# Fifth and sixth expert's weights loaded in pieces, three of six ahead of the last normalised rows

## The reference, cut to what matters

```python
h = rms_norm(x) * (1 + scale1) + shift1
q, k, v, gu, gv = split(h @ w_in)
mix = concat(attention(q, k, v), gelu(gu) * spatial(norm(gelu(gv)))) @ w_out
x = x + gate1 * rms_norm(mix)
h2 = rms_norm(x) * (1 + scale2) + shift2
# router: the best of 4 groups, then the best 2 of its 8 experts
gates = top2_weights(h2 @ router_group, h2 @ router_expert)
hid = silu(h2 @ w_gate[e]) * (h2 @ w_up[e])          # e = 0..31, 1024 -> 256
f = sum_e gates[:, e] * (hid @ w_down[e])            # 256 -> 1024
y = x + gate2 * rms_norm(f)
```

## The kernel before, in words

| place | bytes of which | over what it lies |
|---|---|---|
| w_5 gate | b0 .. b0+8 KB | `h2`, the rows being written to DRAM |
| w_5 up | b0+8 .. +16 KB | `pick_c`, `shift_r`, `shift_b`, `res_t`, most of `w_rs` |
| w_5 down | b0+16 .. +24 KB | rest of `w_rs`, `junk_2`, `mix_g` |
| w_6 gate, up | b0+24 .. +40 KB | `st_bc`, `sel_slot`, `code_oh`, `one_hot` and others of the router |
| w_6d | first 8 KB of the gates' region | `gate_bc[:, 0]`, read until the last tile's `mix_g` |

## Time and profile before

### The profile page before, as it was taken

The page is one execution under the profiler, slowest core; times in us unless marked ns, Lnnn a source line. Parts: engine busy times, 40 slices in busy tenths (PEclk is TensorE's granted clock), DMA queues, the critical chain, the costliest instruction groups (busy, mean ns, idle before and its releaser), DMA issues.

```text
span 671.0 us, 9726 instructions
## 1 busy us (share of the span) xinstructions
PE 548.3 (82%) x3055; PEld 301.5 (45%) x3056; DVE 192.8 (29%) x575; ACT 151.3 (23%) x375; POOL 173.5 (26%) x240
## 2 busy tenths in 40 slices
PE   0479999999987789999997789899998878788700
PEld 0235654444354455455554445455554444444300
DVE  1150312001367763244467102011111111111037
ACT  2630102002126663232221011111111111111142
POOL 1000000002513332143335423334332222221212
PEclk9999999999998999999998899999998898899955
DMA  8999108054199300620044959999999999999183
GB/s 254 401 404 397 65 1 312 1 193 183 37 312 409 124 2 1 219 95 31 33 166 143 409 220 407 395 392 408 405 395 401 402 404 393 406 403 395 47 327 157
DMA packets 53192, 170.23 MB, mean 254 GB/s; under 512 B 7660, under 2 KB 8340, under 8 KB 52256
## 3 DMA queue, kind: packets, MB, share of 16 engines
q1 hardware_dynamic: 46112, 155.45, 60.1%
q0 software_dynamic: 6752, 14.13, 5.9%
q10 hardware_dynamic: 288, 0.13, 0.1%
HBM read 163.23 MB, written 14.58 MB: 265 GB/s over the span
## 4 chain that ended last, share of the span: by engine, by line
PE 54%; DMA 26%; DVE 8%; ACT 4%; SPq 3%; issue 3%; PEld 1%; PEldq 0%; POOL 0%; ACTq 0%; POOLq 0%; DVEq 0%
DMA ring<-in_w_down_dram 12%; PE ps L722 10%; PE ps L619 10%; PE ps L869 8%; PE ps L600 5%; PE ps L520 5%; DMA w<-in_w_down_dram 5%; DMA ring<-in_w_mod_dram 4%; PE ps L877 4%; PE ps L601 3%; PE ps L699 2%; PE ps L539 2%; DMA ring<-in_w_up_dram 2%; ACT probs L1495 2%; DVE probs L1130 1%
## 5 line engine op out<-in xcount | busy, mean ns | idle before, releaser
L869 PE MATMUL ps<-ring,xt 128*64 128x256 f32 x768 | 97.3, 410 | 19.9 <-DMA ring<-in_w_up_dram 12.3
L869 PEld LDWEIGHTS ps<-ring,xt 128*64 128x64 f32 x768 | 64.7, 148 | 58.6 <-issue 36.6
L619 PE MATMUL ps<-ring,h_t 128*128 128x512 f32 x160 | 69.5, 594 | 0.0
L1365 DVE TENSOR_TENSOR hid<-act_g,ps 128x128 f32<-128x128 f32 x32 | 9.2, 287 | 185.7 <-ACT act_g L1572 185.7
L722 PE MATMUL ps<-ring,mix_t 128*128 128x512 f32 x120 | 53.6, 596 | 0.0
L1699 POOL DMA_INDIRECT expert_results<-y_sb,idx_out x32 | 32.7, 1023 | 58.3 <-ACT y_sb L1586 55.4
L619 PEld LDWEIGHTS ps<-ring,h_t 128*128 128x128 f32 x160 | 30.1, 190 | 37.6 <-issue 37.6
L869 PE MATMUL ps<-w,xt 128*64 128x256 f32 x352 | 40.4, 382 | 6.0 <-DMA w<-in_w_up_dram 4.1
L877 PE MATMUL ps<-ring,hid_t 128*64 128x512 f32 x176 | 42.6, 605 | 3.2 <-ACT hid_t L1582 2.6
L600 PE MATMUL ps<-ring,h_t 128*128 128x512 f32 x80 | 42.0, 607 | 2.7 <-DVE h_t L1022 2.7
L1628 POOL TENSOR_TENSOR gm_stats<-gm_stats,half_pow 128x8 f32<-128x8 f32 x5 | 9.7, 1939 | 129.5 <-DVE gm_stats L1088 129.5
(11 more groups left out here) (238 smaller groups left out, 725.5 us busy)
## 6 DMA issues: line engine op xcount, KB each, us to landing
ring<-in_w_mod_dram SPq DMA_DIRECT2D x8, 3072.0 KB, 20.2
ring<-in_w_gate_dram SPq DMA_DIRECT2D x22, 1024.0 KB, 9.3
ring<-in_w_up_dram SPq DMA_DIRECT2D x22, 1024.0 KB, 13.7
ring<-in_w_down_dram SPq DMA_DIRECT2D x22, 1024.0 KB, 16.0
w<-in_w_gate_dram SPq DMA_DIRECT2D x10, 1024.0 KB, 8.6
w<-in_w_up_dram SPq DMA_DIRECT2D x10, 1024.0 KB, 13.6
w<-in_w_down_dram SPq DMA_DIRECT2D x5, 1024.0 KB
w_6d<-in_w_down_dram SPq DMA_DIRECT2D x5, 1024.0 KB, 16.2
```

What stands on the lines that cost most here:

```text
L619: last = pe.matmul(ps[:, 4 + u % 4, :], h_t[:, k, i * P:(i + 1) * P], w[:, k, :], start=(k == 0), stop=(k == KC - 1))
L869: last = pe.matmul(bank[fh * SLOT:(fh + 1) * SLOT, 0:FE].rearrange("p (a f) -> p a f", a=2), x_t[:, k % 4, (k // 4) * SLOT:(k // 4 + 1) * ...
```

## The change

SP's program issues the six loads of experts 4 and 5 one by one, in another order. Right behind expert 3's loads, and ahead of the last tile's `h2` write: expert 5's down after the last `res1` (the gate broadcast is then used up); expert 4's down and up after the last router product and the last squares. The other three stay behind the landing of the rows and of the third gather: expert 4's gate, then expert 5's gate and up. `shift_b`, which lay in the place of expert 4's up, moves to the place of the cosine table. Nothing else differs: the same DMAs of the same sizes, the same instructions on all other engines.

```diff
-        shift_b = sb("shift_b", [P, 2, GROUPS + EXPERTS], F32, b0 + 9 * KB + 160)
+        shift_b = sb("shift_b", [P, 2, GROUPS + EXPERTS], F32, cst_at + 4 * CONST_COLS["cos"][0])
...
+            def load_half(q, c, a):
+                sp.dma_start(weights(c)[0][:, a].rearrange("p (h k) f -> p h (k f)", h=2),
+                             (w_gate, w_up)[a][0, q * WS + c].rearrange("(h p k) f -> p h (k f)", h=2, p=P)
+                             ).then_inc(wgu_in[c % LS], 16)
+
+            def load_down(q, c):
+                sp.dma_start(weights(c)[1], w_down[0, q * WS + c].rearrange("(k p) f -> p k f", p=P)
+                             ).then_inc(wd_in[c % LS], 16)
...
             load_landed(0, 0)
             load_expert(0, RING - 1)
+            load_landed(0, 1)
+            load_landed(0, 2)
+            sp.wait_ge(res1, 2 * TILES)
+            load_down(0, 5)
+            sp.wait_ge(rt_mm, TILES)
+            sp.wait_ge(sq3, 2 * TILES)
+            load_down(0, 4)
+            load_half(0, 4, 1)
             h2_rows(TILES - 1)
 
-            sp.wait_ge(r_both, TILES)
             sp.wait_ge(h2_out[0], 16 * 3)
             sp.wait_ge(h2_out[1], 16 * 2)
             sp.wait_ge(xg_in[XS - 1], 16)
-            load_landed(0, 1)
-            load_expert(0, 4)
+            load_half(0, 4, 0)
 
             sp.wait_ge(rows_made, MAIN_ROWS)
-            load_landed(0, 2)
-            load_expert(0, 5)
+            load_half(0, 5, 0)
+            load_half(0, 5, 1)
```

More of the change, by code:

```diff
@@ L429, in _ @@
                                      ).then_inc(done if hh == 0 else s_wob, 16)
-            def load_expert(q, c):
[L432 to L438, removed]
+            def load_half(q, c, a):
[5 more added lines that the diff above has]
+                             ).then_inc(wd_in[c % LS], 16)
+            def load_expert(q, c):
+                load_half(q, c, 0)
+                load_half(q, c, 1)
+                load_down(q, c)
             def load_landed(q, c):
```

## The result

| what | before | after |
|---|---|---|
| timed runs, median (lowest to highest), 19 each | 674.34 us (669.31 to 676.32) | 677.61 us (675.87 to 680.31) |
| ratio, with its 95% interval | | 1.0049 (1.0035 to 1.0063) |
| the profiled execution's own time | 672.75 us | 678.16 us |
| its span | 671.0 us | 676.3 us |
| mean granted TensorE clock | 0.953 | 0.953 |

The change makes the kernel slower by 0.49%, 3.3 us. The forecast was +0.7 us, 675.4 us in a range of 670.0 to 679.0: the time lies in the range, but 2.2 us above the forecast and outside the forecast's own bounds (up to +2.5 us, 677.2). That it lies in the range is owed to the room made for rival 2, whose mechanism didn't happen. No difference to be measured had the largest chance (0.40), a slower kernel 0.36, and the slower one came.

A forecast was written before the change was run, and what follows sets the result against it. Bound: transfers in the reload stage, whose start hangs on PE finishing expert 0's extra tile. Sum: +4.3 (first rows) + 2.0 (clock) - 2.7 (gather's wait) - 2.9 (clock regained) = +0.7 us, median 675.4 us, range 670.0 to 679.0.

The forecast's parts named there:

- rival 2: Expert 0's extra tile: clock not regained, products stay at 6.12 us; +3.6, 678.3 us (679.2 with 2.9 lost before); chance 0.22.
- The bound: Long stage of 26 reloads is bound by transfers but begins at expert 6's reload, held back by expert 0's extra tile.
- the step from `expert_done(0)` to the end: From expert 6's reload on nothing differs, so a shift of `expert_done(0)` goes through to the end whole.
- The write's landing: Last `h2` write waits in SP's queue behind 3.15 MB, lands at 364.0 instead of 357.9; PE's first rows +4.3 us.
- PE's clock at the first products: After 4.1 us idle PE falls to 1.2 GHz on `products(0)`: +2.0 us, between 0 and 2.9.
- The extra gather and the clock regained: Expert 0's extra tile: gather lands in 3.7 us, PE doesn't wait (-2.7), turn and products back at full clock (-2.9).
- Rival 1: `h2` write not held back by the loads, lands near 359.2, clock stays up: -4.6, 670.1 us; chance 0.15.
- Rival 3: Transfers are the bound, so 3.15 MB earlier saves 7.7 us: 667.0 us; chance 0.03.

The follow-up runs named there:

- the second profile: The changed kernel, unchanged, profiled once more: write to landing 11.8 us, first products 5.28 us, reload of expert 6 at 51.64 us from expert 3's first load.
- The kernel with one load ahead: Changed kernel with only expert 5's down load ahead of the `h2` write, expert 4's down and up behind the gathers: 673.22 us, ratio 0.9974 to before.

## Why the prediction was right or wrong, point by point

**The bound, and the step from `expert_done(0)` to the end.** Right, and shown by the last column of the table.

**The write's landing.** The mechanism was right, its size wrong. I had the write's issue where it was, the loads over at 362.2 and the write's data at 363.5 us; the bulk ended at 365.0, that is 363.7 on the time scale of the profile before. The step that failed is "it lands between 363.5 and 365.0": it landed at 366.8 on that scale, since one DMA engine worked on for 3 us when the others were done. A warning stood behind the row that I used: the gate rows' 16.4 us contained such a tail as well (share 0.47 from 220 to 221 us and 0.13 from 221 to 222), and I read them for the order alone. So +7.7 instead of +4.3 us at PE's first turn. What makes one engine lag isn't shown. The tail was absent with none ahead, some 1.3 us long with one, and 3 us with two and with three, so the landing (2.9, 5.1, 9.7, 11.8 us) doesn't lie on a line of 2.6 us a load. The Trainium skill (DMA: Bandwidth & Descriptors, Latency and other measured facts) says that two of the 16 engines are usually slower than the others in traces; its best guess at the cause concerns DMAs issued by GpSimd, and these loads are SP's. A share of 0.06 agrees with one engine being late; which one it is no run here shows.

**PE's clock at the first products.** Forecast 2.0, measured 1.25 + 0.46 us (products 4.92 for 3.67; from turn to products 2.04 for 1.58), 1.61 in the products of the second profile. Right in size, but giving it back wins nothing: kept busy, PE was ready 1.5 us earlier and then waited 1.68 us, as the extra gather was next. The prediction had PE itself as the last there by 0.3 us, and that held; the margin was too thin for the clock's loss to be won back alone.

**The extra gather and the clock regained.** The changed kernel's extra turn came at L3 + 40.63, 6.6 later than before; as forecast, PE didn't wait, and 2.4 us of the products and 0.4 of the turn came back. The sum with the measured terms: +7.7 + 1.7 - 2.8 - 2.8 = +3.8 us, which is the reload's shift. Against +0.7 the missing 3.1 us are the landing's 3.4, less 0.3 for the clock.

**Rival 2, slower.** Its price, +3.6, is close to the measured 3.3, but its mechanism is not what happened: the clock was regained, the products took 3.67 us. A right number from a wrong reason. **Rival 1** fell: the write was held back. What it imagined, a write that lands early with the loads already moving, came about only when the write was put ahead of them, and then the kernel was faster by 2.6 us and not 4.6, as the first gather pays (6.0 us for 2.9 to 3.3). Its sum also has a slip that changes nothing: by the issue, the loads and the gathers that it adds up the second half ends at 376.2, not 376.4. **Rival 3** fell: the reload came later and nothing was gained from earlier transfers; the sixth's, held back, even helped.

**What I treated as fixed.** I priced the regained clock at the full 2.9 us of one execution. The kernel with one load ahead shows that the same wait costs it in one execution and not in another. Both profiles of the kernel before lost it, so whether the term was too large here stays open; in a forecast of a median it needed a probability of its own.

## What to carry to other kernels

A small transfer that others wait for belongs ahead of bulk loads on the same queue; here it inherited their length, 8.9 us for three loads. Look for the first waiter behind every transfer that a moved load passes, not only for the load's own consumer. An earlier load gains nothing unless what starts the full stage comes earlier; here that hung on a gather, and taking loads out of its way gained 2.6 us, while putting them ahead of the write that it reads from cost 3.3. Split loads by who waits behind them. Fill PE's short waits ahead of critical products, where nothing else is next in line: 3.8 us in the kernel before, nothing in the changed one.

## What the runs showed of the hardware that I had not expected

- One of the 16 DMA engines finishes behind the others after a long row of loads: with two or three loads ahead of the write 3 us at a share of 0.06 to 0.07, 26 or 27 GB/s. The write landed only at the end of this tail, so it counted in full for whoever waited.
- A write on another queue isn't free of a full first queue: 7.6 us to landing against 2.9 alone and 11.8 in line. The first gathers beside loads took 6.0 us against 2.9 to 3.3.
- PE's fall to 1.2 GHz after a wait isn't a function of that wait's length alone: 0.95 us of waiting was followed by products of 5.36 us, 2.65 us by products of 3.67 us and 2.73 us by 5.99 us.
